# Merge stage of a two-block model kernel: first gate weights loaded ahead of the last stored gate tile; the first two output tiles of the projection take their eighth block last

## The chip, the cores and the metric

The kernel runs on one core of a Trainium2 chip. The metric is the device time of one execution in microseconds (us), lower is better. TensorE is written PE below, VectorE DVE, ScalarE ACT, GpSimd POOL; SP is the queue that issues nearly all DMAs.

## What is computed

Two different blocks, each two layers deep, on one sequence of 512 tokens with 1024 channels, all in float32. Both end a layer's mixing part in the same way: several branches (three in the first block, five in the second) are each projected to 1024 channels, multiplied by a sigmoid gate that is itself a projection of the layer's input, summed, and projected once more by `w_out`:

```python
# first block: recurrence, retention, gated unit; then
gate_logits = h @ w_in[l][:, gates]                      # 3 x 1024
merged = sum(sigmoid(gate[n]) * (y[n] @ w_branch[l, n]) for n in range(3))
x = x + merged @ w_out[l]                                # then a conv feed-forward part
# second block: five attentions; then
merge = sigmoid(p['merge'].reshape(B, S, N_BRANCH_2, D_MODEL))
merged = sum(merge * einsum('bsnc,ncd->bsnd', ys, w_branch), axis=2)
return x + merged @ w_out
```

(The branch sums are written here in short form; nothing of the arithmetic is changed by the edit.)

## The kernel before

**Products.** The sequence stands along the free axis (512 columns), channels on the 128 partitions, so a row of 1024 channels is eight tiles, called blocks (`KD` = 8). A float32 product is made of three passes with rounded operands (`block_passes`, L221): high part by high part, high by low, low by high, 128x128 weights against 128x512 activations. One output tile of a 1024-channel projection is 8 blocks of 3 matmuls, 24 matmuls. The weights of a tile arrive by one DMA of 512 KB into a ring of four slots; ACT makes the high part (`weights_high`, a cast of 128x1024) and DVE the low part (`weights_low`, a subtraction). Both parts are kept in two halves, tile n in half n % 2, so the cast of tile n + 2 waits until PE is through with tile n.

**Phases.** The program is a row of phases. A phase ends with a barrier of all engines, SP included (L165, L167 in the trace), and each engine runs its own instruction list in the order written. Waits are on semaphores that are counted up.

**Stored gates.** Some gate tiles are computed as filler between other work in phases before the merge (`Extra`): PE computes a tile into a spare bank, ACT copies it to one of two staging buffers (L1240), SP writes it to memory (`extra_spill`, L1185). `extra_transfers` (L1188) is SP's whole list for this: loads of weights and spills in turn, then the last spills, then a wait for all of them to have landed. In the first block this runs in `branches` (eight tiles, one for each output tile); in the second, five tiles run in `stick_breaking` and nineteen in `attention`.

**The hand-over to the merge.** The merge's first two gate weight tiles are loaded in the phase ahead of it by `load_merge` (L1177) into the ring. In `branches` SP does this after `extra_transfers` has ended (L1312 to L1315), in `attention` too (L2748 to L2750).

**The merge** (`merge`, L1595). For each of eight output tiles: the gate tiles that are not stored, then one tile with all branch weights. DVE multiplies each branch's bank by its gate (L1770) and adds the products up (L1775). At the last output tile ACT and DVE have already split the first seven tiles of the merged sum (`merged_high`, `merged_low`, L274 and L279); the eighth is split after the last addition. Then PE makes the output projection, eight tiles `d` (L1676): tile 0 waits block by block for the split of the merged sum (`m_split`), each tile waits for its weights (`split`), and ends with a count of `projected`. That count releases two things: on ACT the cast of the weights of tile d + 2 (`high`, L1727), on DVE the addition to `x` (L1781), then the low part of tile d + 2 (L1782). `low(count + 1)`, the low part of the second output tile, stands at L1777, behind `merged_low(KD - 1)`.

Of the kernel before, what the change touches and what calls it, by code (L numbers as in the profile page):

```python
# [20 lines left out]
P = 128  # L21
# [1165 lines left out]

def extra_transfers(sp, sems, core, e, begun=False, spilled=0):  # L1188

# [7 lines left out]
    for t in range(e.skip + RING, e.count):  # L1197
        sp.wait_ge(sems["split"], t - RING + 1)
        extra_load(sp, sems, core, e, t)
        spill(t - RING - 2)  # L1200
    for t in range(max(e.count - RING - 2, 0), e.count):
        spill(t)
    for half in range(2):
# [62 lines left out]
def branches(nc, core, b, y_rw, y, y_sg, e, first_gates):  # L1266
# [19 lines left out]
    with phase(nc, *EXTRA, "tables", "qk_landed", "v_landed", "sv_landed", "su_landed", "g_landed", "small_landed", "mean_mm",  # L1286
# [5 lines left out]
        def _(sp):  # L1292
# [17 lines left out]
            for (dst, src), sem in ((tiles(8, 12), "g_landed"), ((small[:, :], b["small1b_dram"]), "small_landed")):  # L1310
                sp.dma_start(dst, src).then_inc(sems[sem], 16)
            extra_transfers(sp, sems, core, e, begun=True, spilled=1)  # L1312
            sp.wait_ge(sems["y_mm"], 2 * NCH)
            for n in range(2):
                load_merge(sp, core, n, 12 * P, KD * P, first_gates(n))  # L1315

# [278 lines left out]
def merge(nc, core, layer, gates, branch, out_units, ys, highs, lows, blocks, merged, gate, part, following, stored, reload, loads=()):  # L1595
# [11 lines left out]
    with nc.sbuf_tensor(f"squares{core.count}", [P, 3, T], F32) as core.squares, \  # L1607
# [47 lines left out]
        def _(pe):  # L1655
# [19 lines left out]
            pe.wait_ge(sems["gated"], KD * own)  # L1675
            for d in range(KD):  # L1676
                n = count + d
                pe.wait_ge(sems["split"], n + 1)
                if d >= 3:
                    pe.wait_ge(sems["x_added"], d - 2)  # L1680
                three_passes(pe, banks[d % 3][:, :], core, n % 2, sems["m_split"] if d == 0 else None).then_inc(sems["projected"], 1)
            sum_channels(pe, sems, core)
# [50 lines left out]
        def _(dve):  # L1733
# [18 lines left out]
            for n in range(count):  # L1752
# [10 lines left out]
                for s in range(n_br):  # L1763
# [7 lines left out]
                    if s:  # L1771
                        dve.wait_ge(sems["taken"], d * n_br + s + 1)
                        if done:
                            dve.wait_ge(sems["added"], done)
                        dve.tensor_tensor(merged[:, d, :], merged[:, d, :], part[:, s % 2, :], ALU.add).then_inc(sems["added"], 1)  # L1775
            merged_low(KD - 1)
            low(count + 1)  # L1777
            dve.wait_ge(sems["reloaded"], 16 * len(reload))
# [934 lines left out]
def attention(nc, core, b, pairs, forgotten, e, first_gates):  # L2713
# [30 lines left out]
    with phase(nc, *EXTRA, "cum_mm", "cum_out", "logit_mm", "masked", "exped", "inverted", "ready", "scaled", "t_mm", "t_out", "pv_mm",  # L2744
               "y_out", "own", "ranked", "replaced") as (block, sems):
        @block.sync
        def _(sp):
            extra_transfers(sp, sems, core, e)  # L2748
            for n in range(2):
                load_merge(sp, core, n, 2 * N_BR2 * P, KD * P, first_gates(n))  # L2750

        @block.tensor
# [367 lines left out]
def block2_layer(nc, core, layer, w, con, tables):  # L3120

    with ExitStack() as outer:
# [35 lines left out]
        with ExitStack() as stack:  # L3158
            b["cum"], b["stats"] = buf(stack, "cum", [2, T]), buf(stack, "stats", [3, 6])
            with ExitStack() as scratch:  # L3160
# [59 lines left out]
                for m in range(2):  # L3220
# [3 lines left out]
                    [(slot, 2 if n >= 0 else 0) for n in range(-2, 4 * len(pairs) + 3) for slot in (("early", n), n)],  # L3224
                    core.banks[7:8], [core.ring[:, n * T:(n + 1) * T] for n in range(2)]), gates)
                core.slots = core.ring
# [156 lines left out]
```

## Time and profile before

| | us |
|---|---|
| median of three runs | 3456.91 |
| lowest, highest | 3454.43, 3463.46 |
| profiled execution, its own time | 3468.01 |
| span of the profiled execution | 3466.2 |
| PE busy in the span | 3339.1 (96%) |
| DVE, ACT busy | 1893.7 (55%), 1434.7 (41%) |
| granted PE clock, mean | 0.977 of full speed |

PE is busy for 96% of the span, so time is lost or won where PE stands still or runs at half clock. There are 1.8 us between the span and the execution's own time. The stages that the change touches, by the trace: the first block's merges begin at 409.7 and 1374.9 us, the second's at 2508.5 and 3258.9 us, and the attention phases ahead of the latter at 2273.4 and 3021.5 us.

### The profile page before, as it was taken

The numbers are of one execution on the slowest core, as the hardware profiler recorded it, in microseconds if no ns is written. First come the engines' busy times: TensorE is split into PE (matmuls) and PEld (weight loads), VectorE is DVE, ScalarE is ACT, GpSimd is POOL, SyncE is SP. The second block draws the span as 40 slices with busy tenths as digits, with TensorE's granted clock in tenths as the row PEclk, the third lists the DMA queues.
The fourth block names the chain that finished last, engine by engine and source line by source line (L and its number), as shares of the span: only waits on it lengthen the run. The fifth ranks groups of instructions, "written<-read, shape, count | busy, mean of one in ns | idle before, by whom it ended". The sixth has DMA issues, their size and how long they took to land. (4 is left out here: it accounts for less than half of the span.)

```text
span 3466.2 us, 53876 instructions
## 1 busy us (share of the span) xinstructions
PE 3339.1 (96%) x21860; PEld 2612.1 (75%) x21860; DVE 1893.7 (55%) x3265; ACT 1434.7 (41%) x2357; POOL 58.5 (2%) x44
## 2 busy tenths in 40 slices
PE   8999999999999999999999999899899999999898
PEld 6777688788877876887888778566587787566686
DVE  6645644677566446346773552367555632376555
ACT  6423423444254235234443333545533333555532
POOL 0110000000000100000000000000000000000000
PEclk9999999999999999999999999899999999999999
DMA  4324232223232233322233252122152432121341
GB/s 157 95 67 172 101 116 89 91 95 111 86 131 89 76 127 138 114 85 98 96 106 101 103 166 89 40 89 77 47 179 95 154 115 104 51 74 59 129 138 67
DMA packets 106534, 356.86 MB, mean 103 GB/s; under 512 B 12545, under 2 KB 12929, under 8 KB 103489
## 3 DMA queue, kind: packets, MB, share of 16 engines
q1 hardware_dynamic: 106304, 353.67, 30.0%
q8 instruction: 160, 2.62, 0.3%
q14 instruction: 70, 0.57, 0.1%
HBM read 308.93 MB, written 38.80 MB: 100 GB/s over the span
## 5 line engine op out<-in xcount | busy, mean ns | idle before, releaser
L224 PE MATMUL banks<-h_high,weights_high 128*128 128x512 f32 x2464 | 993.2, 403 | 27.8 <-DVE weights_low L245 19.9
L225 PE MATMUL banks<-h_low,weights_high 128*128 128x512 f32 x2464 | 969.3, 393 | 0.0
L226 PE MATMUL banks<-h_high,weights_low 128*128 128x512 f32 x2464 | 968.4, 393 | 0.0
L224 PEld LDWEIGHTS banks<-h_high,weights_high 128*128 128x128 f32 x2464 | 466.5, 189 | 141.4 <-DVE weights_low L245 21.2
L226 PEld LDWEIGHTS banks<-h_high,weights_low 128*128 128x128 f32 x2464 | 466.3, 189 | 102.6
L225 PEld LDWEIGHTS banks<-h_low,weights_high 128*128 128x128 f32 x2464 | 467.0, 190 | 97.1 <-issue 3.3
L217 DVE TENSOR_TENSOR weights_low<-ring,weights_high 128x1024 fp32r<-128x1024 f32 x134 | 167.1, 1247 | 304.4 <-ACT weights_high L212 303.6
L1689 ACT CAST weights_high<-ring 128x1024 fp32r<-128x1024 f32 (+2 forms) x124 | 140.7, 1134 | 456.8 <-PE banks L226 456.4
L1737 DVE TENSOR_TENSOR weights_low<-ring,weights_high 128x1024 fp32r<-128x1024 f32 (+2 forms) x124 | 164.6, 1327 | 294.3 <-ACT weights_high L1689 294.2
L212 ACT CAST weights_high<-ring 128x1024 fp32r<-128x1024 f32 x134 | 140.4, 1048 | 367.4 <-PE banks L226 362.3
L1865 ACT CAST weights_high<-ring 128x1024 fp32r<-128x1024 f32 (+1 forms) x116 | 132.6, 1143 | 334.4 <-PE banks L226 334.4
L1912 DVE TENSOR_TENSOR weights_low<-ring,weights_high 128x1024 fp32r<-128x1024 f32 (+1 forms) x116 | 154.9, 1335 | 93.7 <-ACT weights_high L1865 93.4
L224 PE MATMUL banks<-h_high,extra_high 128*128 128x512 f32 x384 | 169.4, 441 | 1.2 <-ACT ring L1240 1.2
L225 PE MATMUL banks<-h_low,extra_high 128*128 128x512 f32 x384 | 152.8, 398 | 0.0
L224 PE MATMUL banks<-y_high,weights_high 128*128 128x512 f32 x352 | 136.9, 389 | 0.0
L225 PE MATMUL banks<-y_low,weights_high 128*128 128x512 f32 x352 | 136.9, 389 | 0.0
L226 PE MATMUL banks<-y_high,weights_low 128*128 128x512 f32 x352 | 136.9, 389 | 0.0
L224 PE MATMUL banks<-ffn_high,weights_high 128*128 128x512 f32 x352 | 136.9, 389 | 0.0
L225 PE MATMUL banks<-ffn_low,weights_high 128*128 128x512 f32 x352 | 136.9, 389 | 0.0
L226 PE MATMUL banks<-ffn_high,weights_low 128*128 128x512 f32 x352 | 136.9, 389 | 0.0
L226 PE MATMUL banks<-h_high,extra_low 128*128 128x512 f32 x304 | 120.4, 396 | 0.0
L224 PEld LDWEIGHTS banks<-h_high,extra_high 128*128 128x128 f32 x384 | 72.9, 190 | 47.2 <-issue 36.2
(454 smaller groups left out, 5057.0 us busy)
## 6 DMA issues: line engine op xcount, KB each, us to landing
ring<-in_in SPq DMA_DIRECT2D x136, 512.0 KB, 3.7
ring<-in_up SPq DMA_DIRECT2D x88, 512.0 KB, 3.2
ring<-in_gates SPq DMA_DIRECT2D x68, 512.0 KB, 3.7
x<-in_gates SPq DMA_DIRECT2D x60, 512.0 KB, 3.9
ring<-in_down SPq DMA_DIRECT2D x32, 704.0 KB, 4.1
ring<-in_out SPq DMA_DIRECT2D x32, 512.0 KB, 3.2
ring<-in_branch SPq DMA_DIRECT2D x16, 768.0 KB, 4.4
stored<-g_spill SPq DMA_DIRECT2D x16, 768.0 KB, 4.5
```

What stands on the lines that cost most here:

```text
L212: act.copy(core.wh[:, half, 0:width], slot(core, s[0], s[1])[:, 0:width]).then_inc(sems["rounded"], 1)
L217: dve.tensor_tensor(core.wl[:, half, 0:width], slot(core, s[0], s[1])[:, 0:width], core.wh[:, half, 0:width].bitcast(F32), ALU.subtract).t ...
L224: pe.matmul(bank, core.wh[:, half, w], high, start=start, stop=False)
L225: pe.matmul(bank, core.wh[:, half, w], low, start=False, stop=False)
L226: return pe.matmul(bank, core.wl[:, half, w], high, start=False, stop=stop)
L1689: act.copy(core.wh[:, n % 2, 0:width(n)], place(n)).then_inc(sems["rounded"], 1)
L1737: dve.tensor_tensor(core.wl[:, n % 2, 0:width(n)], place(n), core.wh[:, n % 2, 0:width(n)].bitcast(F32), ALU.subtract).then_inc(sems["spli ...
L1865: act.copy(core.wh[:, n % 2, 0:width(n)], place(n)).then_inc(sems["rounded"], 1)
L1912: dve.tensor_tensor(core.wl[:, n % 2, 0:width(n)], place(n), core.wh[:, n % 2, 0:width(n)].bitcast(F32), ALU.subtract).then_inc(sems["spli ...
```

## The change

Five edits:

1. `extra_transfers` gets a parameter `before_last`, a function called ahead of the spill of the last tile. In `branches` this function waits for `y_mm` and issues the two merge loads, which stood behind everything else before.
2. In `attention` the two merge loads stand ahead of `extra_transfers`, as the first DMAs of the phase.
3. Since they now lie in the ring during the whole attention phase, the two staging buffers move: one to another place of the ring, one to the tile `kc_vc`.
4. PE makes the output projection in the order: blocks 0 to 6 of tile 0, blocks 0 to 6 of tile 1, block 7 of tile 0, block 7 of tile 1, then tiles 2 to 7 as before.
5. DVE makes the low part of the second output tile's weights, `low(count + 1)`, ahead of `merged_low(KD - 1)`.

```diff
-def extra_transfers(sp, sems, core, e, begun=False, spilled=0):
+def extra_transfers(sp, sems, core, e, begun=False, spilled=0, before_last=None):
...
     for t in range(max(e.count - RING - 2, 0), e.count):
+        if t == e.count - 1 and before_last is not None:
+            before_last()
         spill(t)
...
-            extra_transfers(sp, sems, core, e, begun=True, spilled=1)
-            sp.wait_ge(sems["y_mm"], 2 * NCH)
-            for n in range(2):
-                load_merge(sp, core, n, 12 * P, KD * P, first_gates(n))
+            def merge_weights():
+                sp.wait_ge(sems["y_mm"], 2 * NCH)
+                for n in range(2):
+                    load_merge(sp, core, n, 12 * P, KD * P, first_gates(n))
+
+            extra_transfers(sp, sems, core, e, begun=True, spilled=1, before_last=merge_weights)
...
-            for d in range(KD):
+            for d, first, end in ((0, 0, KD - 1), (1, 0, KD - 1), (0, KD - 1, KD), (1, KD - 1, KD), *((d, 0, KD) for d in range(2, KD))):
                 n = count + d
                 pe.wait_ge(sems["split"], n + 1)
                 if d >= 3:
                     pe.wait_ge(sems["x_added"], d - 2)
-                three_passes(pe, banks[d % 3][:, :], core, n % 2, sems["m_split"] if d == 0 else None).then_inc(sems["projected"], 1)
+                for k in range(first, end):
+                    if d == 0:
+                        pe.wait_ge(sems["m_split"], k + 1)
+                    mm = block_passes(pe, banks[d % 3][:, :], core, n % 2, k, core.hh[:, k, :], core.hl[:, k, :], k == 0, k == KD - 1)
+                if end == KD:
+                    mm.then_inc(sems["projected"], 1)
...
+            low(count + 1)
             merged_low(KD - 1)
-            low(count + 1)
...
-            extra_transfers(sp, sems, core, e)
             for n in range(2):
                 load_merge(sp, core, n, 2 * N_BR2 * P, KD * P, first_gates(n))
+            extra_transfers(sp, sems, core, e)
...
-                    core.banks[7:8], [core.ring[:, n * T:(n + 1) * T] for n in range(2)]), gates)
+                    core.banks[7:8], [core.ring[:, 5 * T - P:6 * T - P], p[:, tl["kc_vc"], :]]), gates)
```

**SP at the end of `branches`, first layer, before.** L1185 is a spill, L1179 a merge load, L1627 the first load of the merge phase:

```order
L1185 DMA g_spill<-gate_staging 128x512 [waits evacuated_a] x7
L1179 DMA ring<-in_gates 128x1024 [waits y_mm_a,spilled1_a,spilled0_a]
L1179 DMA ring<-in_gates 128x1024
L165 UNCONDITIONAL_BRANCH
L1622 UNCONDITIONAL_BRANCH [waits barrier_Pool_Activation_PE_DVE_SP_release]
```

The same place after:

```order
L1185 DMA g_spill<-gate_staging 128x512 [waits evacuated_a] x6
L1179 DMA ring<-in_gates 128x1024 [waits y_mm_a]
L1179 DMA ring<-in_gates 128x1024
L1185 DMA g_spill<-gate_staging 128x512 [waits evacuated_a]
L165 UNCONDITIONAL_BRANCH [waits spilled1_a,spilled0_a]
```

The loads moved ahead of the last spill and no longer wait for `spilled`; the end of the phase does.

**PE at the start of the output projection, first layer of the first block, before:** the last two blocks of tile 0 and the first matmuls of tile 1.

```order
L224 MATMUL banks<-h_high,weights_high 128x512 [waits m_split_b]
L225 MATMUL banks<-h_low,weights_high 128x512
L226 MATMUL banks<-h_high,weights_low 128x512
L224 MATMUL banks<-h_high,weights_high 128x512 [waits m_split_b]
L225 MATMUL banks<-h_low,weights_high 128x512
L226 MATMUL banks<-h_high,weights_low 128x512
L224 MATMUL banks<-h_high,weights_high 128x512 [waits split_b]
```

After: the seventh block of tile 1, the eighth of tile 0, the eighth of tile 1, the first matmul of tile 2.

```order
L224 MATMUL banks<-h_high,weights_high 128x512
L225 MATMUL banks<-h_low,weights_high 128x512
L226 MATMUL banks<-h_high,weights_low 128x512
L224 MATMUL banks<-h_high,weights_high 128x512 [waits m_split_b,split_b]
L225 MATMUL banks<-h_low,weights_high 128x512
L226 MATMUL banks<-h_high,weights_low 128x512
L224 MATMUL banks<-h_high,weights_high 128x512 [waits split_b]
L225 MATMUL banks<-h_low,weights_high 128x512
L226 MATMUL banks<-h_high,weights_low 128x512
L224 MATMUL banks<-h_high,weights_high 128x512 [waits split_b]
```

Tile 0 ends three matmuls ahead of tile 2's first one, where it ended 24 matmuls ahead of it.

**DVE at the same place, before,** from the last product and sum of the merge on:

```order
L1770 TENSOR_TENSOR y_rw<-stored,banks 128x512
L1775 TENSOR_TENSOR y_rs<-y_rs,y_rw 128x512
L279 TENSOR_TENSOR h_low<-y_rs,h_high 128x512
L1737 TENSOR_TENSOR weights_low<-ring,weights_high 128x1024
L1781 TENSOR_TENSOR x<-x,banks 128x512
L1737 TENSOR_TENSOR weights_low<-ring,weights_high 128x1024
```

After (the file's lines are ten higher here):

```order
L1780 TENSOR_TENSOR y_rw<-stored,banks 128x512
L1785 TENSOR_TENSOR y_rs<-y_rs,y_rw 128x512
L1747 TENSOR_TENSOR weights_low<-ring,weights_high 128x1024
L279 TENSOR_TENSOR h_low<-y_rs,h_high 128x512
L1791 TENSOR_TENSOR x<-x,banks 128x512
L1747 TENSOR_TENSOR weights_low<-ring,weights_high 128x1024
```

Two neighbours changed places; both still stand behind the last sum.

**SP at the start of `attention`, first layer of the second block, before** (L1163 loads weights for a stored gate):

```order
L2746 UNCONDITIONAL_BRANCH
L1163 DMA x<-in_gates 128x1024 x7
L1185 DMA g_spill<-ring 128x512
L1163 DMA x<-in_gates 128x1024
L1185 DMA g_spill<-ring 128x512
```

After:

```order
L2756 UNCONDITIONAL_BRANCH
L1179 DMA ring<-in_gates 128x1024 x2
L1163 DMA x<-in_gates 128x1024 x7
L1185 DMA g_spill<-ring 128x512
L1163 DMA x<-in_gates 128x1024
L1185 DMA g_spill<-others 128x512
```

The weights of the first stored gates of this phase are now the third and the fourth transfer of the queue.

## Rows read from the trace of the kernel before

**Rows 1.** Timeline, end of `branches`, layer 0: start, duration, engine, line, [idle before <-releaser].

```profile
402.90 0.32 SPq L1185 DMA_DIRECT2D g_spill<-gate_staging  x1
...
403.76 0.69 DVE L1591 TENSOR_TENSOR y_rs<-y_rs,p_rs 128x512 f32<-128x512 f32 x1
404.95 0.81 SPq L1179 DMA_DIRECT2D ring<-in_gates  x2
406.49 0.33 SPq L1627 DMA_DIRECT2D ring<-in_branch  x1
...
408.80 0.40 ACT L235 CAST weights_high<-ring 128x256 fp32r<-128x256 f32 x1 [5.93 <-DMA ring<-in_gates]
...
409.72 0.79 PE L224 MATMUL banks<-h_high,weights_high 128*128 128x512 f32 x1 [7.47 <-DVE weights_low L245]
```

**Rows 2.** Timeline, the same place in layer 1, PE.

```profile
1374.92 0.80 PE L224 MATMUL banks<-h_high,weights_high 128*128 128x512 f32 x1 [7.41 <-DVE weights_low L245]
```

**Rows 3.** Timeline, start of the second block's first merge.

```profile
2507.59 0.40 ACT L235 CAST weights_high<-ring 128x256 fp32r<-128x256 f32 x1 [2.73 <-PEq L167]
...
2508.51 0.50 PE L224 MATMUL banks<-h_high,weights_high 128*128 128x512 f32 x1 [2.50 <-DVE weights_low L245]
```

**Rows 4.** Stretches: length, busy time (instructions) of each engine, granted clock (PEclk), DMA.

```profile
409.72:415.00 5.28, 5.28 (x13) 4.13 (x14) 4.84 (x7) 5.19 (x10) 0.00 (x0) 0.50 1.03 407
...
2658.70:2664.30 5.60, 5.60 (x13) 4.39 (x14) 3.00 (x3) 1.58 (x2) 0.00 (x0) 0.50 0.35 112
...
2508.50:2512.00 3.50, 3.50 (x15) 2.93 (x16) 3.24 (x4) 3.50 (x7) 0.00 (x0) 1.00 1.07 360
```

**Rows 5.** Timeline, output projection of the first block's first merge.

```profile
564.63 0.39 PE L224 MATMUL banks<-h_high,weights_high 128*128 128x512 f32 x1
...
567.13 0.69 DVE L1775 TENSOR_TENSOR y_rs<-y_rs,y_rw 128x512 f32<-128x512 f32 x1
...
570.39 0.50 PE L224 MATMUL banks<-h_high,weights_high 128*128 128x512 f32 x1
...
575.99 0.39 PE L224 MATMUL banks<-h_high,weights_high 128*128 128x512 f32 x1
...
576.19 1.06 ACT L1689 CAST weights_high<-ring 128x1024 fp32r<-128x1024 f32 x1 [4.31 <-PE banks L226]
...
577.27 1.23 DVE L1737 TENSOR_TENSOR weights_low<-ring,weights_high 128x1024 fp32r<-128x1024 f32 x1 [0.40 <-ACT weights_high L1689]
```

**Rows 6.** Timeline, output projection of the second block's first merge.

```profile
2656.58 0.69 DVE L1775 TENSOR_TENSOR queries<-queries,part 128x512 f32<-128x512 f32 x1
...
2658.70 0.80 PE L224 MATMUL banks<-h_high,weights_high 128*128 128x512 f32 x1 [3.70 <-DVE h_low L279]
...
2667.59 0.39 PE L224 MATMUL banks<-h_high,weights_high 128*128 128x512 f32 x1
```

**Rows 7.** Line L1163 at 2274.7 us: the fourth load of the first attention.

```profile
L1163 SPq DMA_DIRECT2D x<-in_gates x1: 432/432/432, 2274.7 to 2274.7; - x1
...
DMA to landing us min/median/max: 6.7/6.7/6.7
```

**Rows 8.** Timeline, opening of the first attention phase.

```profile
2278.06 1.04 ACT L1230 CAST extra_high<-x 128x1024 fp32r<-128x1024 f32 x1 [0.38 <-DMA x<-in_gates]
...
2279.01 1.08 ACT L2844 ACTIVATE queries<-banks 128x512 f32<-128x512 f32 x2
...
2282.35 0.60 ACT L2844 ACTIVATE cum<-banks 128x512 f32<-128x512 f32 x1 [1.56 <-PE banks L2799]
...
2283.64 0.49 PE L2762 MATMUL banks<-others,queries 64*128 64x128 f32 x4 [0.68 <-DVE stats L2871]
```

**Rows 9.** Line L1163 at 3023.9 us: the fourth load of the second attention.

```profile
L1163 SPq DMA_DIRECT2D x<-in_gates x1: 432/432/432, 3023.9 to 3023.9; - x1
...
DMA to landing us min/median/max: 5.6/5.6/5.6
```

**Rows 10.** Timeline of ACT, opening of the second attention phase.

```profile
3032.16 0.60 ACT L2844 ACTIVATE cum<-banks 128x512 f32<-128x512 f32 x1 [1.56 <-PE banks L2799]
```

## The prediction, as put on record

> **What bounds the kernel now.** By the profile's table PE is busy for 96% of the span, so I read the stages around the edits for one thing only: where PE stands still, and what ends that. The views, in this order: the waits at the merge's start, the timeline there, the stretches with their granted clock, the timeline of the output projection in both blocks, and the opening of the attention phases.
>
> At the start of the first block's merges PE is idle for 7.47 and 7.41 us [rows 1, 2]. The reader sees a row of serial steps in [rows 1]: the last spill is issued at 402.90, SP then waits, issues the two merge loads at 404.95, starts the next phase at 406.49, and ACT waits for the first of these loads until 408.80, which is 5.93 us of idle time put down to that DMA. At the start of the second block's merges the idle time is 2.50 us, and ACT did not wait for a DMA [rows 3]: the loads, though issued late in the phase, had long landed there. In the output projection PE is idle for 3.70 us in the second block [rows 6] and hardly at all in the first, where tile 1 begins at 570.39 and 24 matmuls before that start tile 0 had begun at 564.63 [rows 5]. At the attention phase's opening ACT's work on four banks (L2844) holds up the first mask, and with it PE's logits at 2283.64 [rows 8].
>
> **Part 1: the merge loads ahead of the last spill (edit 1).** The last spill starts as before, since the loads are issued before the tile it waits for is ready; no engine waits for SP there. SP's next step at 404.95 was the first load; now it goes to the barrier. From the end of the two issues (404.95 + 0.81 = 405.76) to the first DMA of the next phase at 406.49 are 0.73 us; counted from 404.95 the next phase begins at 405.68. DVE's last row ends at 404.45, so the spill's landing stays the last event. ACT is released by the same barrier, so its first cast can begin at 405.7; PE followed 0.92 us behind ACT in both places, 409.72 - 408.80 [rows 1] and 2508.51 - 2507.59 [rows 3]. PE starts at 406.6 and not 409.7: **3.1 us gained in each of two layers, 6.2 us**. Behind this the casts and subtractions of the merge follow ACT's and DVE's start and move with it. If the two engines' own barrier work hides part of it, the low end is 2.2 us each; the high end, 3.2 us, is what ACT's idle time in [rows 1] has beyond that in [rows 3], 5.93 less 2.73.
>
> What is left idle is some 4.4 us. In the stretch behind the old gap PE ran at half clock for 5.28 us, 13 matmuls; at the full clock 15 took 3.50 us [rows 4]. So the slow stretch cost about 2.3 us, and the like stretch in the second block, after only 3.70 us of idle time, cost 2.6 [rows 4, 6]. A gap of 4.4 us lies above 3.70, so I leave this cost where it is and count nothing.
>
> **Part 2: the merge loads first in `attention` (edit 2).** At the far end it gains nothing, since no DMA was waited for there [rows 3]. At the opening it puts two transfers of 512 KB ahead of the first stored gates' weights. These take the places of the third and fourth load. The fourth was issued at 2274.7 and took 6.7 us to land, 2281.4 [rows 7]. ACT needs two casts of 1.04 us and then four operations of L2844, two of which take 1.08 us together, the fourth one ending at 2282.95 [rows 8]. Now: second cast 2281.4 to 2282.5; the four, at a pace of 0.49 us, end at 2284.5. This is 1.5 us later, and the mask, PE's logits and all that follows shift by it: **1.5 us lost in layer 0**. In layer 1 the fourth load landed at 3023.9 + 5.6 = 3029.5 [rows 9]; casts to 3030.6, the fourth L2844 could start at 3032.0, and it started at 3032.16 anyway, held by PE [rows 10]: **nothing lost in layer 1**, with 0.1 us to spare. Bounds for each layer: 0 (all hidden) and 3.1, the further wait if the two transfers delayed these loads by twice that.
>
> The Trainium skill, page "DMA: Bandwidth & Descriptors", section "Rules for kernel authors", advises the opposite of a worry: issue a DMA early and wait for it late, so its fixed cost overlaps. By that rule this part would cost nothing. The trace agrees as far as the merge's own loads go; for the loads queued behind them ACT's wait says otherwise.
>
> **Part 3: the moved staging buffers (edit 3).** The same copies and spills to other addresses: nothing, hidden beside PE. A copy that ran slower would show only if PE waited for its bank, which has a whole tile's matmuls to be emptied.
>
> **Part 4: the order of the output projection (edits 4 and 5).** What the order shows decides it. Tile 1 needs its low part, and that still stands behind the last sum on DVE. In the second block the last sum ends at 2657.27 [rows 6]; the low part then takes 1.22 us, to about 2658.45. PE stands waiting as before and resumes at 2658.46 for 2658.70: **0.2 us gained**, at half clock worth 0.1. So the 3.70 us are not filled: they are only waited for in front of tile 1 and not in front of block 7.
>
> The other end is new. Tile 0 now ends three matmuls ahead of tile 2, and the weights of tile 2 may be cast only when tile 0 has ended. First block [rows 5]: PE begins at 564.63; at 0.229 us a matmul the 45th, tile 0's last, starts at 574.7 and ends at 575.1; tile 1 ends three later, 575.8. From tile 0's end: ACT 0.04 + 1.06, DVE 0.02 + 1.23, PE 0.05, in all 2.4 us, to 577.5, where tile 2 began at 575.99 before. DVE's low part of tile 1 is made from 567.8 to 569.1, in time for PE at 569.4. **1.5 us lost in each layer.** Second block [rows 6]: tile 2 began at 2667.59; now matmul 28 after the restart would come at 2667.46, tile 0 ends at 2666.93, tile 2 begins 2.4 later, 2669.3. **1.7 us lost in each layer.** Sum 2 x 1.5 + 2 x 1.7 = 6.4 us. Bounds: 0, if the cast were ready in time, and 2.4 each, if the addition to `x` (0.69 us on DVE) came in between. From tile 3 on, each tile has 5.5 us of matmuls for 3 us of splitting, and all is as before.
>
> **Sum.** -6.2 + 1.5 + 6.4 = +1.7 us on the profiled 3468.0 (span 3466.2 and 1.8 around it). That execution lies 11.1 us above the median; the steps are the same in all, so I put the difference on the median: 3456.9 + 1.7, rounded to **3458.5 us**. A measurement of this kernel can tell about 0.3%, 10.4 us, from no change.
>
> **The rivals.**
>
> *The new stops bring the half clock.* PE now stops for about 1.7 us ahead of tile 2 in four places, and at the attention's opening for 0.68 + 1.5 = 2.2 us. In [rows 6, 4] a gap of 3.70 us is followed by 5.60 us of half clock; behind the gap of 2.50 us the clock stayed full [rows 3, 4]. If each of the five stops halves the clock for a stretch of about 3.4 us (a third less than the 5.28 measured), each costs 1.5 us: up to 7.5, a total of +9.2, 3466 us; with two of them 3461.5. It is decided by whether a gap of 1.7 us counts, and the 2.50 us gap speaks against it. The Trainium skill, page "TensorE: Matmul & The Clock Gate", section "What's actually happening", calls the number of slow matmuls variable from run to run; by that the same stop may cost in one execution and not in the next. Slower than before by 4 to 9 us: chance 0.2.
>
> *The shorter gap at the merge keeps the clock.* If 4.4 us of idle time no longer halved it, 2.3 us in each layer come on top: 1.7 - 4.6 = -2.9, 3454 us. Against it speaks the gap of 3.70 us, which did. 0.1.
>
> *The exchange fills the gap, as its form suggests.* Were tile 1's weights split before the last sum, PE would work through the 3.70 us and keep the clock (2.6 more): 2 x 6.3 = 12.6 gained in the second block, 1.7 - 12.6 = -10.9, 3446 us. The order of DVE, which shows the low part behind L1775, speaks against it. 0.05.
>
> *The early opening of attention is free* (by the rule cited above, or since PE makes it up later in the phase): +0.2, 3457 us. 0.15.
>
> *The loads are early but the phase is not*: something else of the phase's end, a barrier or the merge's next DMAs, holds ACT until about 408. Then part 1 gives nothing: +7.9, 3465 us. 0.05.
>
> **How the numbers follow.** The forecast holds with 0.45, from 3455 to 3461 with an uncertainty of the medians of some 3 us. With the rivals' 3454 and 3466 the range is 3451 to 3466; outside it lie the filled gap and the worst of the clock. Faster by over 0.3% is the third rival and little else: 0.06. Slower by over 0.3%, at or above 3467.3, needs all clock stops and bad luck: 0.05. The rest, 0.89, is within 0.3%.
>
> **What would show it.** Right: PE idle at the first block's merge 4.4 us instead of 7.47, ACT's L235 with no DMA in its wait; in the projection a new stop of 1.7 us ahead of tile 2 in all four merges, released by the low part of the weights, and the old 3.7 us in the second block still there, some 0.2 shorter; the fourth L2844 of the first attention ending 1.5 us later after the phase's start. Wrong: the old projection gap gone, tile 2 starting without a stop, or more stretches at half clock than before.

## The result, and the profile after

| kernel | median us (runs) | ratio to before, 95% interval | in us |
|---|---|---|---|
| before, beside it | 3461.0 (11) | | |
| changed | 3465.0 (11) | 1.0019 [1.0010, 1.0028] | +6.6 [+3.5, +9.7] |

Beside the changed kernel the kernel before took 3461.0 us and not 3456.9, so the forecast is compared by the difference: +1.7 us forecast, +6.6 measured. The +6.6 comes from the ratio, which is taken over all runs; the two medians are 4.0 us apart. In the runs below too the us behind a ratio are worked out from it, and can differ from the medians by some us.

The hand-over did what was forecast. The openings and the output projection both cost more than forecast, and in both half clock was found that the sum had at nothing. Half clock means here a granted clock of 0.50, the lower of TensorE's two levels (1.2 and 2.4 GHz).

**The hand-over (part 1).** The changed kernel's timeline at the place of [rows 1]; columns as there.

```profile
403.07 0.33 SPq L1185 DMA_DIRECT2D g_spill<-gate_staging  x1
...
403.92 0.69 DVE L1596 TENSOR_TENSOR y_rs<-y_rs,p_rs 128x512 f32<-128x512 f32 x1
...
405.87 0.33 SPq L1632 DMA_DIRECT2D ring<-in_branch  x1
...
405.88 0.40 ACT L235 CAST weights_high<-ring 128x256 fp32r<-128x256 f32 x1 [2.84 <-PEq L167]
...
406.80 0.50 PE L224 MATMUL banks<-h_high,weights_high 128*128 128x512 f32 x1 [4.38 <-DVE weights_low L245]
```

Between the last spill and the next phase's first DMA SP issues nothing any more. ACT waits 2.84 us for the barrier and no longer for a DMA, and PE's stop is 4.38 us for 7.47 [rows 1], 4.36 for 7.41 in layer 1 [rows 2]: the 3.1 us of the forecast.

**The output projection (part 4).** First block, then second block, first layer each.

```profile
573.60 0.50 PE L224 MATMUL banks<-h_high,weights_high 128*128 128x512 f32 x1 [1.72 <-DVE weights_low L1747]
```

```profile
2657.99 0.80 PE L224 MATMUL banks<-h_high,weights_high 128*128 128x512 f32 x1 [3.47 <-DVE weights_low L1747]
...
2668.90 0.50 PE L224 MATMUL banks<-h_high,weights_high 128*128 128x512 f32 x1 [1.72 <-DVE weights_low L1747]
```

A stop of 1.72 us ahead of tile 2 where there was none [rows 5, 6], and the 3.70 us of [rows 6] shortened to 3.47. One row of the groups of instructions adds them up. Its columns are busy time, mean ns and idle time before, with what ended most of it; before first, then changed.

```profile
L224 PE MATMUL banks<-h_high,weights_high 128*128 128x512 f32 x2464 | 993.2, 403 | 27.8 <-DVE weights_low L245 19.9 <-DVE h_low L279 7.4 <-DVE weights_low L217 0.2
```

```profile
L224 PE MATMUL banks<-h_high,weights_high 128*128 128x512 f32 x2464 | 994.6, 404 | 29.9 <-DVE weights_low L1747 13.8 <-DVE weights_low L245 13.8 <-ACT gate_staging L1243 1.9
```

The 6.1 us gained at L245 (19.9 to 13.8) are spent at L1747: 13.8 = 4 x 1.72 + 2 x 3.47, where the old gap had 7.4. (The 1.9 us behind `gate_staging` are stops early in `branches`; traces of kernels without edit 1 have them too, e2_order for 2.3 us.)

**The opening of attention (part 2).** Changed kernel, layer 0, then layer 1, against [rows 8, 10].

```profile
2276.83 1.04 ACT L1233 CAST extra_high<-x 128x1024 fp32r<-128x1024 f32 x1 [10.58 <-DMA x<-in_gates]
2278.10 1.05 ACT L1233 CAST extra_high<-x 128x1024 fp32r<-128x1024 f32 x1 [0.22 <-DMA x<-in_gates]
2279.05 1.08 ACT L2854 ACTIVATE queries<-banks 128x512 f32<-128x512 f32 x2
2280.02 1.08 ACT L2854 ACTIVATE cum<-banks 128x512 f32<-128x512 f32 x2
...
2281.79 0.80 PE L2772 MATMUL banks<-others,queries 64*128 64x128 f32 x4 [2.75 <-DVE stats L2881]
```

```profile
3038.68 0.49 PE L2772 MATMUL banks<-others,queries 64*128 64x128 f32 x4 [3.22 <-DVE stats L2881]
```

PE's stop of 0.68 us [rows 8] became 2.75 and 3.22. What followed it in layer 0 is in the stretches (us, busy time of PE, PEld, DVE, ACT, POOL, granted clock, DMA share, GB/s):

```profile
2281.80:2285.00 3.20, 3.20 (x10) 2.49 (x11) 2.78 (x15) 1.61 (x9) 0.00 (x0) 0.50 0.50 168
2285.50:2290.00 4.50, 4.50 (x24) 3.46 (x23) 4.06 (x21) 1.51 (x7) 0.00 (x0) 1.00 0.00 0
```

The stretch right behind the stop ran at half clock, the next one at the full clock. Taken between the same barriers, the attention phase took 237.58 us for 234.17 in layer 0 (+3.4) and 238.11 for 236.39 in layer 1 (+1.7), where 1.5 and 0 had been forecast.

The profiled executions differ by 9.8 us (3476.0 to 3466.2), more than the medians. 3.1 of it is in the phase behind the second block's first merge, whose instructions the change leaves as they were. The changed kernel first, then the kernel before in the same window:

```profile
2838.40:2844.80 6.40, 6.40 (x16) 5.05 (x17) 1.11 (x2) 2.35 (x5) 0.00 (x0) 0.50 0.26 82
```

```profile
2838.40:2844.80 6.40, 6.40 (x32) 5.22 (x31) 1.39 (x2) 2.10 (x5) 0.00 (x0) 1.00 0.25 84
```

The work is that of `project2`, the second block's projections; PE was busy for all of the 9 us ahead of it. Of the fourteen traces eight have half clock at this place, some 131 us into the phase: all three with stops ahead of tile 2 and e3_attention, which has none, for 6.8 us, and four others for 3.4 us. So it needs no new stop ahead of it; whether one makes it likelier stays open. Single traces are read below for stops and for stretches right behind them, and costs are taken from repeated runs.

### The profile page after: what moved, and what is told of

Same layout as the page of the kernel before. It is cut to its first block and busy times, and to the rows that moved or that the text cites. A ratio compares the mean times of both kernels' runs of the same rounds, so it can differ in the third digit from the quotient of the medians.

```text
span 3476.0 us, 53884 instructions
## 1 busy us (share of the span) xinstructions
PE 3344.2 (96%) x21860; PEld 2617.3 (75%) x21860; DVE 1893.4 (54%) x3265; ACT 1433.9 (41%) x2357; POOL 58.5 (2%) x44
## 5 line engine op out<-in xcount | busy, mean ns | idle before, releaser
L224 PE MATMUL banks<-h_high,weights_high 128*128 128x512 f32 x2464 | 994.6, 404 | 29.9 <-DVE weights_low L1747 13.8
L1747 DVE TENSOR_TENSOR weights_low<-ring,weights_high 128x1024 fp32r<-128x1024 f32 (+2 forms) x124 | 164.6, 1327 | 292.5 <-ACT weights_high L1699 292.3
```

Of the source, the lines that this page charges most:

```text
L224: pe.matmul(bank, core.wh[:, half, w], high, start=start, stop=False)
L1747: dve.tensor_tensor(core.wl[:, n % 2, 0:width(n)], place(n), core.wh[:, n % 2, 0:width(n)].bitcast(F32), ALU.subtract).then_inc(sems["spli ...
```

## Each part alone

My theory after this result, A: hand-over and order do what the forecast said, and the opening was under-sized: the loads land later than taken, and the stop that this makes has a half-clock stretch behind it. The rivals are B, the sizes were right and the excess is chance; C, something is given back later or lies in the staging buffers; and in each run one more that is named there.

**The hand-over alone (e1_branches).** The changed kernel's edit 1, nothing else:

```diff
     for t in range(max(e.count - RING - 2, 0), e.count):
+        if t == e.count - 1 and before_last is not None:
+            before_last()
         spill(t)
```

> Edit 1 alone: the merge loads ahead of the last spill in the first block, everything else as before. Theory A (each step costs what its own stretch of the trace shows; the step that was mis-sized is the opening of the attention phases): PE idle at the start of the first block's merges 4.4 us instead of 7.5, the half-clock stretch behind it as long as before or shorter, 6 us less in all (ratio about 0.998). Theory B (the sizes on record are right and the rest of the loss is half-clock stretches that fall by chance): the same 6.2 us here. Theory C (the earlier start is given back later in the merge, by transfers that the merge waits for): PE idle 4.4 us, but the time within 2 us of before.

Measured: ratio 0.9980 [0.9970, 0.9991], -7 us [-10, -3]. The stops are 4.38 and 4.37 us. In its trace the two merges of the first block are 3.10 and 2.75 us shorter and the two phases ahead of them 0.98 and 0.27. The 6.2 us of the forecast hold, and nothing is given back later.

**The order alone (e2_order).** Edits 4 and 5:

```diff
-            for d in range(KD):
+            for d, first, end in ((0, 0, KD - 1), (1, 0, KD - 1), (0, KD - 1, KD), (1, KD - 1, KD), *((d, 0, KD) for d in range(2, KD))):
...
+            low(count + 1)
             merged_low(KD - 1)
-            low(count + 1)
```

> Edits 4 and 5 alone: the new order of the output projection. Theories A and B: a stop of 1.7 us ahead of tile 2 in all four merges, the old stop of 3.7 us in the second block only 0.2 us shorter, 6.4 us more in all (ratio about 1.002). The rival that the exchange fills the stop: 3.7 us and a half-clock stretch less in each of the second block's merges, ratio below 0.997.

Measured: 1.0026 [1.0015, 1.0037], +9 us [+5, +13]. Four stops of 1.72 and two of 3.47 us, to a hundredth those of the changed kernel. The exchange doesn't fill the gap. The forecast of +6.4 is inside the interval, but low in it.

**The openings alone (e3_attention).** Edits 2 and 3:

```diff
-            extra_transfers(sp, sems, core, e)
             for n in range(2):
                 load_merge(sp, core, n, 2 * N_BR2 * P, KD * P, first_gates(n))
+            extra_transfers(sp, sems, core, e)
```

> Edits 2 and 3 alone: merge loads first in the attention phases, staging buffers moved. Theory A: PE stops for 2.7 to 3.2 us at the opening of both attention phases instead of 0.7, with a half-clock stretch behind each; 2.1 us of stop and 1.5 us of clock in the first, 1 us and up to 1.5 us in the second: 5 us more (ratio about 1.0015). Theory B: 1.5 us more in the first, nothing in the second (ratio 1.0004, not to be told from 1). Rival D: the moved staging buffers slow copies or transfers along the phase; then the phases are longer by more than the opening shows.

Measured: 1.0009 [1.0000, 1.0018], +3.1 us [0, +6.2]. That lies between theory A's 5 and theory B's 1.5 and excludes neither. The trace shows stops of 2.27 and 1.28 us, the first with half clock behind it, the second without; theory A had expected 2.7 to 3.2 us and half clock in both. Against before the attention phases are 2.96 us longer and 0.09 us shorter. Of the kernels below, e11_cut_full has the same two loads ahead, and its two phases are 2.94 and 2.86 us longer.

**The same two loads behind the first loads (e5_behind).** Staging buffers as changed, and:

```diff
-            extra_transfers(sp, sems, core, e)
+            extra_first_loads(sp, sems, core, e)
             for n in range(2):
                 load_merge(sp, core, n, 2 * N_BR2 * P, KD * P, first_gates(n))
+            extra_transfers(sp, sems, core, e, begun=True)
```

> Edits 2 and 3, but with the two merge loads behind the four first weight loads of the attention phase instead of ahead of them. Theory A (the place in the queue is what costs): the opening is as before, PE stops for 0.7 us, ratio 1.000 within 0.0005. Rival D (staging buffers, or the 1 MB of extra transfers in the opening as such): still 2 us or more per phase over before.

Measured: 0.9993 [0.9984, 1.0002], -2.4 us [-5.5, +0.7]; attention phases +0.00 and +0.20 us, both stops 0.68 us. With the loads in the queue but behind the four, the cost is gone: it is the place in the queue and not the transfers.

**The staging buffers alone (e4_staging)**, edit 3:

```diff
-                    core.banks[7:8], [core.ring[:, n * T:(n + 1) * T] for n in range(2)]), gates)
+                    core.banks[7:8], [core.ring[:, 5 * T - P:6 * T - P], p[:, tl["kc_vc"], :]]), gates)
```

> Edit 3 alone: the two staging buffers of the stored gates' spills in the attention phases lie at other addresses, everything else as before. Theory A (part 3 of the prediction: the same copies and spills, nothing): the attention phases are as long as before to 0.3 us apart from half-clock stretches, PE's stop at the first opening is 0.68 us, the median within 3 us of before. Rival (the other buffers cost or gain, and with them the -1.5 us seen with the loads behind the first loads): a difference of over 3 us, and copies of 128x512 that last longer or PE waiting for their banks.

Measured: 1.0002 [0.9992, 1.0011], +0.7 us [-2.8, +3.8]. A copy (L1240) takes 584 or 585 ns in its trace as against 586 before; the attention phases are -0.01 and +0.19 us longer. Part 3 holds, and rival C has no place there.

**One load ahead, one behind (e6_one_ahead)**, staging buffers as changed.

> The attention phase with one of the two merge loads ahead of the four first loads and the other behind them (edit 3 as well; the branches and the order as in the kernel before). Theory A: each transfer put ahead costs the opening in proportion, since the loads land one after the other in the order in which they are issued. One ahead: the second stored gate's half-tile lands one place later than before, ACT's second cast begins some 1 us later, PE's first stop of the phase in layer 0 is about 1.4 us, between 0.68 (none ahead) and 2.3 to 2.75 (both ahead). Phase +0.7 us in layer 0 without a half-clock stretch, +2.2 with one; median +0 to +3 against before. Rival B (the opening is not held by the loads, what was measured with both ahead is chance): no change of the stop, 0.7 us. Rival C (the first of the two carries all the delay): stop of 2.3 us or more and a half-clock stretch behind it, +3 us.

Measured: 1.0006 [0.9996, 1.0016], +2.1 us [-1.4, +5.5]. The stop is 0.68 us, so my expectation of 1.4 was wrong. ACT in the first opening, with the loads behind (e5_behind), with one ahead (e6_one_ahead) and with both ahead (e3_attention):

```profile
2271.40 1.05 ACT L1230 CAST extra_high<-x 128x1024 fp32r<-128x1024 f32 x1 [0.25 <-DMA x<-in_gates]
...
2275.68 0.60 ACT L2845 ACTIVATE cum<-banks 128x512 f32<-128x512 f32 x1 [1.56 <-PE banks L2800]
2276.85 0.32 ACT L2820 ACTIVATE probs<-probs,stats 128x31 f32<-128x31 f32 x1 [0.58 <-DVE stats L2872]
```

```profile
2275.90 1.05 ACT L1230 CAST extra_high<-x 128x1024 fp32r<-128x1024 f32 x1 [0.59 <-DMA x<-in_gates]
...
2278.64 0.60 ACT L2845 ACTIVATE cum<-banks 128x512 f32<-128x512 f32 x1 [0.23 <-PE banks L2800]
2279.82 0.32 ACT L2820 ACTIVATE probs<-probs,stats 128x31 f32<-128x31 f32 x1 [0.58 <-DVE stats L2872]
```

```profile
2274.84 1.05 ACT L1230 CAST extra_high<-x 128x1024 fp32r<-128x1024 f32 x1 [0.21 <-DMA x<-in_gates]
...
2278.42 0.32 ACT L2819 ACTIVATE probs<-probs,stats 128x31 f32<-128x31 f32 x1 [0.58 <-DVE stats L2871]
```

The phases begin at 2266.65, 2269.62 and 2266.63 us. The second cast starts 4.8, 6.3 and 8.2 us into the phase, and the first probabilities 10.2, 10.2 and 11.8. So the first transfer put ahead delays the cast by 1.5 us and is paid out of ACT's slack: its wait for PE's fourth bank shrinks from 1.56 to 0.23 us. The second one finds only 0.2 us left. The cost is no share for each transfer but what lies beyond the slack; in the changed kernel the first probabilities come 12.3 us into the phase, 2.1 later than before.

In layer 1 the room that [rows 10] seem to leave depended on the clock. The kernel before, then e8_early_low (further down; the opening is the same code), each from 1.3 us behind the start of the phase:

```profile
3022.80:3026.10 3.30, 3.30 (x8) 2.11 (x7) 0.00 (x0) 0.88 (x1) 0.00 (x0) 0.50 0.88 287
```

```profile
3012.80:3016.10 3.30, 3.30 (x15) 2.25 (x14) 0.17 (x1) 1.04 (x1) 0.00 (x0) 1.00 0.97 364
```

At half clock PE's first logits came 12.0 us into the phase, at the full clock 10.3. The changed kernel had the full clock there too, and its logits came at 12.9.

## The order, cut elsewhere

**Cut behind block 3 of tile 1 (e7_order74).**

```diff
-            for d, first, end in ((0, 0, KD - 1), (1, 0, KD - 1), (0, KD - 1, KD), (1, KD - 1, KD), ...
+            for d, first, end in ((0, 0, KD - 1), (1, 0, 4), (0, KD - 1, KD), (1, 4, KD), ...
```

> Edits 4 and 5 with another cut: PE takes blocks 0 to 6 of tile 0, blocks 0 to 3 of tile 1, the eighth block of tile 0 and then blocks 4 to 7 of tile 1, so tile 0 ends 12 matmuls ahead of tile 2 and not 3. Everything else as before. Theory A (the stop ahead of tile 2 is the 2.4 us from tile 0's end to its release, less the matmuls that lie in between): 12 matmuls are 2.75 us, the four stops of 1.72 us are gone, the gap of 3.5 us in the second block stays; the median is that of before, -2 to +1 us, against +9 (3.9 to 12.8) with the order of the change. Rival B (what costs is the swap on DVE or the splitting of a tile's eight blocks, not the stop): the loss of about +9 stays. Rival C (the stop was filled but the half-clock stretches come anyway): +2 to +4.

Measured: 0.9993 [0.9984, 1.0002], -2.4 us [-5.5, +0.7]. The stops are gone. The same row of its trace:

```profile
L224 PE MATMUL banks<-h_high,weights_high 128*128 128x512 f32 x2464 | 994.1, 403 | 28.3 <-DVE weights_low L245 19.5 <-DVE weights_low L1742 6.9 <-ACT gate_staging L1240 1.6
```

6.9 = 2 x 3.47: only the second block's gaps are left. Rival B, that the swap on DVE or the cut as such costs, falls: both are in this kernel.

**The changed kernel with its loads behind (e10_behind_full), with the other cut (e11_cut_full), and with both (e12_both_full).**

> The changed kernel with one thing undone: the two merge loads of the attention phases go behind the four first loads (edits 1, 3, 4 and 5 as changed). Theory A (the opening costs the changed kernel the shift of the first probabilities and the half-clock stretch that follows the stop, +3.4 and +1.7 us in its trace): no stop over 0.9 us at the openings, phases as before, and the median 3 to 5 us below the changed kernel's, +1 to +4 against before. Rival B (the opening was priced rightly at 1.5 us and the excess of the change over the prediction is in the order of the output projection): 1 to 2 us below the changed kernel, +4 to +6 against before.

> The changed kernel with another cut of the output projection: blocks 0 to 3 of tile 1 ahead of tile 0's eighth block, blocks 4 to 7 behind it, all else as changed. Theory A (the order costs by its stop ahead of tile 2, 1.72 us in each of four merges, with or without a half-clock stretch): the four stops are gone, the 3.47 us gap of the second block stays, 7 to 9 us below the changed kernel, -2 to 0 against before. Rival B (the stop costs less than its length, as most of it is made up later): 3 us or less below the changed kernel. Rival C (the order had been under-sized): 11 us or more below.

> The changed kernel with both of these: merge loads of the attention phases behind the four first loads, and the cut behind block 3 of tile 1. What is left is edit 1, the other staging buffers and a gap that is 0.2 us shorter. Theory A (three separate terms that add: -7 from the hand-over, +3 to +5 from the openings, +7 to +9 from the order): -6.5 to -9 against before, 3452 to 3455 us. Rival B (a term of its own in the staging buffers or in the combination, which no single edit shows): -4 or less of a gain.

Measured against before: e10_behind_full 1.0005 [0.9996, 1.0014], +1.7 us [-1.4, +4.8]; e11_cut_full 0.9982 [0.9973, 0.9991], -6.2 [-9.3, -3.1]; e12_both_full 0.9968 [0.9955, 0.9980], -11 [-16, -7]. So the openings cost the changed kernel some 5 us (+6.6 to +1.7, as A said; with an uncertainty of 4 us this doesn't exclude B's 1 to 2). Its order cost 12.8 us between e11_cut_full and the changed kernel, 12.8 between e12_both_full and e10_behind_full, and 11.4 between e7_order74 and e2_order, each uncertain by 4 to 6. By the medians the three are 8.8, 9.0 and 13.8. My range of 7 to 9 is at the low edge of this, and rival C of that run, 11 or more, is as near. In e12_both_full the gains add, at least as A said; its rival B falls.

Where that lies: the sums over the four merges, between their barriers (length, then PE's busy time, which grows when the same matmuls run at half clock). First e2_order and e7_order74, then the changed kernel and e11_cut_full, then e10_behind_full and e12_both_full.

```profile
sum 817.96, PE 784.63 PEld 646.92 DVE 394.15 ACT 277.15 POOL 0.00; mean PE 196.16 PEld 161.73 DVE 98.54 ACT 69.29 POOL 0.00
```

```profile
sum 807.52, PE 781.00 PEld 644.93 DVE 394.91 ACT 277.11 POOL 0.00; mean PE 195.25 PEld 161.23 DVE 98.73 ACT 69.28 POOL 0.00
```

```profile
sum 814.83, PE 785.61 PEld 647.76 DVE 394.17 ACT 276.90 POOL 0.00; mean PE 196.40 PEld 161.94 DVE 98.54 ACT 69.22 POOL 0.00
```

```profile
sum 800.68, PE 778.30 PEld 642.76 DVE 394.88 ACT 276.87 POOL 0.00; mean PE 194.58 PEld 160.69 DVE 98.72 ACT 69.22 POOL 0.00
```

```profile
sum 810.88, PE 781.64 PEld 644.46 DVE 394.15 ACT 276.85 POOL 0.00; mean PE 195.41 PEld 161.11 DVE 98.54 ACT 69.21 POOL 0.00
```

```profile
sum 801.99, PE 779.63 PEld 643.83 DVE 394.89 ACT 276.90 POOL 0.00; mean PE 194.91 PEld 160.96 DVE 98.72 ACT 69.23 POOL 0.00
```

Length less busy time is idle time: 33.3 and 26.5, 29.2 and 22.4, 29.2 and 22.4. The pairs differ by 6.8 to 6.9 us, four times 1.72, as much as the stops. The rest, 3.6, 7.3 and 2.0 us, is busy time: the kernels with the stops had more half clock in their merges, in all three pairs. It does not stand right behind the stops (no half-clock stretch follows any of the 12 that the traces show).

Part of it stands some 35 us later, at the merge's end, where PE stops for 1.58 us in every kernel and then runs the 16 small matmuls of the next norm's sums (L330). Changed kernel, then e11_cut_full, first merge:

```profile
608.16 2.71 PE L330 MATMUL banks<-ones,squares 128*128 128x1 f32 x16 [1.58 <-ACT squares L311]
```

```profile
607.02 1.92 PE L330 MATMUL banks<-ones,squares 128*128 128x1 f32 x16 [1.58 <-ACT squares L311]
```

These 16 take 1.92 us in 40 of the 44 merges of the eleven kernels without the stops, all twelve with the other cut among them, and 2.1 to 2.3 in the other four. In nine of the twelve merges with the stops they take 2.2 to 3.0 us: the half clock begins 2.1 to 3.6 us ahead of the merge's last barrier there, and with the other cut at most 1.3 us ahead of it. In the three pairs this makes 2.2, 2.8 and 1.3 of the 3.6, 7.3 and 2.0 us. What is left is largest in the second pair, where both gaps of 3.47 us have 6.8 us of half clock with them in the changed kernel, and in e11_cut_full one has 3.4 and the other none. How far the whole sum moves from kernel to kernel is seen in the changed kernel and e10_behind_full, whose merges are the same code: 785.6 and 781.6 us busy. Why the half clock at the norm comes earlier in kernels with the stops stays open.

**The exchange done so that it fills the gap (e8_early_low), and with the hand-over (e9_best).** This is the third rival of the prediction, built: in the second block DVE makes tile 1's low part ahead of the last sums.

```diff
                 for s in range(n_br):
+                    if n == count - 1 and n_br == 5 and s == 2:
+                        for k in range(KD - 1):
+                            merged_low(k)
+                        low(count + 1)
...
+            ((0, 0, KD - 1), (1, 0, 5), (0, KD - 1, KD), (1, 5, KD)) if n_br == 5 else ((0, 0, KD), (1, 0, KD))
```

> Second block only (the first block is as before): DVE makes the low parts of blocks 0 to 6 of the merged activations and then the low part of tile 1's weights behind the first two of the last tile's gate products, ahead of its other sums; PE takes blocks 0 to 6 of tile 0, 0 to 4 of tile 1, the eighth block of tile 0, the last three of tile 1. Theory A (the 3.7 us gap stood because tile 1's low part stood behind the last sum on DVE): PE has 36 matmuls, 8.2 us, to work while DVE ends the sums; the gap of 3.7 us and the half-clock stretch behind it (1.3 us or more) are gone in both layers and no stop comes ahead of tile 2 beyond 0.3 us: -3.7 to -6 us for each merge, -7 to -12 in all, 3449 to 3454 us. Rival B (the gap is made by the sums, and moves to the place where PE needs block 7): some 3 us of gap stay in front of tile 0's eighth block, median -1 to 0. Rival C (DVE's work in front of the sums delays the last sum more than PE's extra work covers): slower, +2 to +4.

> The early low part of the second block (as in the run of that name) with edit 1 of the change, nothing else. Theory A: both gains add, -6.5 from the branches' end and -7 to -12 from the second block: -13 to -18 us, ratio 0.995 to 0.996, 3443 to 3448 us. Rival B (the exchange gains nothing): -6.5, ratio 0.998. Rival C (a gain of one is given back by the other through half-clock stretches): less than the sum of the two by 3 us or more.

Measured: e8_early_low 0.9978 [0.9968, 0.9987], -7.6 us [-11, -4.5]; e9_best 0.9961 [0.9947, 0.9975], -13.5 us [-18, -9], 3447.1 against 3461.7 us. DVE and PE of e8_early_low, the place of [rows 6]:

```profile
2647.26 1.22 DVE L1742 TENSOR_TENSOR weights_low<-ring,weights_high 128x1024 fp32r<-128x1024 f32 x1
...
2651.77 0.69 DVE L1784 TENSOR_TENSOR queries<-queries,part 128x512 f32<-128x512 f32 x1
```

```profile
2653.98 0.47 PE L224 MATMUL banks<-h_high,weights_high 128*128 128x512 f32 x1 [0.16 <-DVE h_low L279]
```

The low part is made 4.5 us before the last sum, PE works through, and of 3.70 us 0.16 are left. Without half clock behind it the merges took 192.1 us each, for 197.7 and 197.9 before. That is 11.4 us less in one pair of traces; the repeated runs give 7.6, inside the 7 to 12 expected. With the hand-over the two gains add (13 to 18 expected). e9_best is faster than both kernels of this case.

## Why the prediction was wrong

The main step that failed put half clock at nothing in the sum. The prediction let the new stops cost their length alone, because one stop of 2.50 us had the full clock behind it [rows 3]. In part 2 a second one failed with it: the shift of the openings, 1.5 us in layer 0 and nothing in layer 1, measured 2.1 and 0.9. The idle time of the output projection was right.

- **Part 1, the hand-over: right.** -6.2 forecast, -7 measured alone, and both stops as computed. "I leave this cost where it is" was a little too careful: behind the stops of 4.4 us half clock went on for 4.1 us on average (12 stops), behind those of some 7 us for 4.9 (16 stops).
- **Part 2, the openings: failed.** +1.5 forecast, +3.1 [0, +6.2] measured alone and some +5 by taking it out of the changed kernel. Three things in it were mis-sized.
  - The shift in layer 0. I took the landings of the old third and fourth loads, 8.1 us into the phase for the later one (2281.4 by [rows 7], in a phase that began at 2273.33), and ACT's second cast started at 8.7. With ACT's four operations behind it the first probabilities came 2.1 us later, not 1.5.
  - The shift in layer 1, taken as nothing because PE held ACT anyway [rows 10]. It did so until 10.7 us into the phase, in layer 0 until 9.0, and the half-clock stretch shown under e6_one_ahead lies between. PE's first logits came 0.9 us later than before, and 2.6 later than in e8_early_low at the same clock.
  - The half clock. The stop had a half-clock stretch behind it in five of six openings with both loads ahead. In the changed kernel the slow 3.20 us above hold 10 matmuls and the next 4.50 us 24, so 3.1 and 5.3 in one us.
- **Part 3: right**, +0.7 us [-2.8, +3.8] for nothing.
- **Part 4, the order: stops and idle time right, size low.** The stop of 1.7 us in four places, the 3.7 us gap still there and 0.2 shorter, both released by the weights' low part, as written. In the first block I had 1.5 us: the 0.229 us a matmul of that sum stands in no row, [rows 5] give (575.99 - 570.39) / 24 = 0.233, and with it the step comes to 1.7. The idle time of the sum was right all the same (6.4 forecast; the stops' 6.9 less 0.5 of the old gap). But the order cost +9 us [+5, +13] alone, and 11 to 13 (9 to 14 by medians) against the other cut. In the traces the difference is the merges' busy time, 2.0 to 7.3 us more with the stops, of which 1.3 to 2.8 is half clock at the merge's end. It was not in the sum.
- **The rival that the new stops bring half clock**, given 0.2, is the one in whose range the measured +6.6 lies. Its price of 1.5 us a stretch fits (3.20 us at half clock is 1.6 us lost). Its places were half right: the openings, but not right behind the stops ahead of tile 2. I spoke against it by one stop of 2.50 us. That was one draw: the same stop had half clock behind it in 10 of 28 cases. The kernel's spread of some 10 us is as large as the whole difference, so that +6.6 falls in this range is in part luck; the counts of stretches speak for the mechanism, not the total.
- **The rules of the Trainium skill that were cited.** The Trainium skill, page "DMA: Bandwidth & Descriptors", section "Rules for kernel authors", says to issue a DMA early and wait for it late. As the prediction read it, this part would have cost nothing. Here one transfer ahead was free, out of 1.3 us of slack, and the second was not; for the loads queued behind, the measurement decides. The Trainium skill, page "TensorE: Matmul & The Clock Gate", section "What's actually happening", calls the number of slow matmuls variable from run to run; the counts below agree.

## What to carry to other kernels

A load issued early can delay what stands behind it in its queue (here the second cast, by 1.5 us for one load ahead and 3.4 for two): put it behind the loads that the phase's opening waits for, and count the opening's slack before putting anything ahead. A split of a reduction that makes a tile end shortly before its buffers are needed again trades one wait for another: measure the path from the tile's end to its buffers' release (here 2.4 us), and leave that much work between. And an exchange on one engine gains little if both neighbours stand behind the same late step (0.2 us of 3.7 here); moved ahead of that step, the same work removed the gap. Last, room read from one trace may belong to a half-clock stretch of that trace: look at the granted clock of the stretch before counting on it.

## What the runs showed of the hardware

Of the stops that the edits touch, the longer ones had half clock behind them more often, and the same stop had it in some traces and not in others. Counted in the fourteen traces (a case is a stop with a stretch at 0.50 that begins in it or within 3.5 us of its end):

| stop of PE | half clock behind it |
|---|---|
| 0.68 us, attention's opening | 0 of 22 |
| 1.72 us, ahead of tile 2 | 0 of 12 |
| 1.28 to 3.22 us, attention's opening | 5 of 6 |
| 2.50 us, second block's merge start | 10 of 28 |
| 3.47 to 3.71 us, second block's projection | 20 of 24 |
| 4.36 to 4.39 us, hand-over with edit 1 | 12 of 12 |
| 6.94 to 7.48 us, hand-over without it | 16 of 16 |

Length is not all of it: a stop of 1.68 us at an opening had half clock behind it and twelve of 1.72 us ahead of tile 2 had none. The norms' stops of 1.58 to 1.74 us (L330), which no edit touches, had it in 78 of 84 cases. What PE does ahead of and behind these stops differs, and no run separates that from the length. I had not expected half clock inside PE's unbroken work either, as at 2838.40 above. Executions of one kernel spread over some 10 us, and by the stretches above a single trace can't price an edit of a few us.
